# Attention of a hybrid decoder step: 160 transpose groups in 76 steps in place of 88, with a fifth copy buffer

## What is computed

```python
def nsa_core(q, qpos, gates, cmp_kv, fetch, n_sel, win_kv, win_pos):
    s = einsum(qg, cmp_kv[:, :, 0]) - slopes * d_c
    p_cmp = masked_softmax(s, d_c >= 0)
    o_cmp = einsum(p_cmp, cmp_kv[:, :, 1])
    ...
    _, idx = lax.top_k(score, min(TOP_K, n_sel))
    sel = fetch(idx)
    ...
    o_slc = einsum(masked_softmax(s, d_s >= 0), vsel)
    ...
    o_win = einsum(masked_softmax(s, mask_w), win_kv[:, :, 1])
    o = g[:, :, 0] * o_cmp + g[:, :, 1] * o_slc + g[:, :, 2] * o_win
```

## Time and profile before

| | us |
|---|---|
| median of 3 runs | 1759.17 |
| lowest and highest | 1758.44, 1761.16 |
| the profiled execution | 1755.95 |
| its span | 1754.3 |
| attention stage in the trace | 506 to 840.5 |
| matmuls busy in that stage | 315.5 of 334 |

### The profile page before, as it was taken

The page is one execution under the profiler, slowest core; times in us unless marked ns, Lnnn a source line. Parts: engine busy times, 40 slices in busy tenths (PEclk is TensorE's granted clock), DMA queues, the critical chain, the costliest instruction groups (busy, mean ns, idle before and its releaser), DMA issues.

```text
span 1754.3 us, 35862 instructions
## 1 busy us (share of the span) xinstructions
PE 1706.9 (97%) x13523; PEld 1584.2 (90%) x13523; DVE 1211.5 (69%) x1805; ACT 801.9 (46%) x1462; POOL 836.7 (48%) x862
## 2 busy tenths in 40 slices
PE   8999999999989999999999999999999999999998
PEld 7999998999966666667998999999999999999998
DVE  6789965879777677767548754455596979745435
ACT  5311325565876666667325333333433333315335
POOL 2202965555524343444454656665664545326521
PEclk9999999999999999999999999999999999999999
DMA  5323346655533443442414323332584643341114
GB/s 163 123 64 81 88 149 163 187 155 145 137 98 96 145 123 115 128 135 60 148 49 153 111 98 108 111 111 99 178 263 144 180 146 120 103 128 55 49 37 147
DMA packets 179723, 214.61 MB, mean 122 GB/s; under 512 B 22940, under 2 KB 150664, under 8 KB 174799
## 3 DMA queue, kind: packets, MB, share of 16 engines
q1 hardware_dynamic: 174333, 196.30, 36.4%
q0 software_dynamic: 4032, 13.40, 2.6%
q10 hardware_dynamic: 1186, 2.63, 0.5%
HBM read 181.30 MB, written 35.59 MB: 124 GB/s over the span
## 4 chain that ended last, share of the span: by engine, by line
PE 51%; DVE 9%; issue 3%; ACT 3%; DMA 2%; POOL 2%; SPq 1%; ACTq 0%; DVEq 0%; POOLq 0%
PE ps L2825 11%; PE ps L3208 6%; PE ps L2830 5%; PE ps L2583 5%; PE ps L201 3%; PE ps L3213 3%; PE ps L1984 3%; PE ps L1997 3%; PE ps L1970 3%; PE ps L3721 2%; DVE S L2238 2%; PE ps L2024 2%; POOL S L1924 2%; PE ps L207 2%; SPq L3083 1%
## 5 line engine op out<-in xcount | busy, mean ns | idle before, releaser
L1924 POOL TENSOR_SCALAR S<-S,inv,gate_p 128x640 f32<-128x640 f32 (+7 forms) x186 | 124.2, 684 | 187.3 <-DVE inv L2248 187.3
L1311 DVE SCALAR_TENSOR_TENSOR y<-u,conv_w,y 128x1024 f32<-128x1024 f32 x120 | 156.0, 1346 | 1.2
L3208 PE MATMUL ps<-dn_op_hi,dn_hi 128*128 128x264 f32 x672 | 136.8, 285 | 3.8 <-DVE dn_op_lo L3256 3.8
L3208 PE MATMUL ps<-dn_op_lo,dn_hi 128*128 128x264 f32 x672 | 135.7, 283 | 0.0
L659 POOL COPY relaid<-raw 128x512 f32<-128x512 f32 x128 | 83.5, 683 | 87.5 <-PE ps_p L1083 39.3
L2121 ACT ACTIVATE S<-S,mn 128x64 f32<-128x64 f32 (+8 forms) x180 | 108.7, 609 | 1.2 <-DVE mn L2238 1.2
L3139 POOL TENSOR_TENSOR dn_lo<-dn_t_sum,dn_hi 128x512 fp32r<-128x512 f32 x48 | 77.2, 1610 | 65.9 <-ACT dn_hi L3161 65.7
L3208 PEld LDWEIGHTS ps<-dn_op_hi,dn_hi 128*128 128x128 f32 x672 | 103.7, 188 | 5.3 <-DVE dn_op_lo L3256 5.1
L1012 PE MATMUL ps_p<-Ahi,win_hi 128*128 128x352 f32 x456 | 104.1, 328 | 1.5 <-DVE Alo L1288 1.5
L2825 PE MATMUL ps<-s_hi,up_hi 128*128 128x264 f32 x512 | 104.1, 285 | 0.0
L3208 PEld LDWEIGHTS ps<-dn_op_lo,dn_hi 128*128 128x128 f32 x672 | 103.9, 188 | 0.0
(11 more groups left out here) (494 smaller groups left out, 5052.1 us busy)
## 6 DMA issues: line engine op xcount, KB each, us to landing
s_raw<-in_cache_slc_kv_dram SPq DMA_DIRECT2D x256, 128.0 KB, 2.1
raw<-in_cache_cmp_kv_dram SPq DMA_DIRECT2D x188, 128.0 KB, 3.7
dn_op_raw<-hidden SPq DMA_DIRECT2D x21, 1056.0 KB, 6.5
hidden<-cs SPq DMA_DIRECT2D x32, 528.0 KB, 2.6
up_raw<-in_w_up_dram SPq DMA_DIRECT2D x16, 1024.0 KB, 5.4
dn_w<-in_w_down_dram SPq DMA_DIRECT2D x48, 256.0 KB, 4.9
win_raw<-in_w_in_dram SPq DMA_DIRECT2D x38, 256.0 KB, 3.3
raw<-in_cache_cmp_kv_dram POOLq DMA_DIRECT2D x64, 128.0 KB, 3.7
```

The lines of the kernel that those rows point to most:

```text
L1311: i = V_.scalar_tensor_tensor(out=y, in0=x, scalar=w, in1=y, op0=ALU.mult, op1=ALU.add)
L1924: nc.gpsimd.tensor_scalar(x, x, inv[:, n % 3, 3 * e + br:3 * e + br + 1], c.gate_p[:, i, H * br + h:H * br + h + 1], ALU.mult, ALU.mult).t ...
L3208: nc.tensor.matmul(ps[:, 2 * m + j, 0:HC], w_hi[q % 4][:, k, :], x[:, k, HC * j:HC * j + HC], start=(k == 0 and x is op_hi[n]), stop=False)
```

## The change

A unit of 5 or 7 groups (i = 3, 6 and 7) now ends in a step of three groups, so that its steps are 2+3 or 2+2+3. Units of 3 groups (i = 1) keep their 2+1. There are 76 steps. Since a step of three can follow one of two before its `pv` is done, there are five `PT` tiles, and the fifth lies where small sampled tiles were; some of these go to two free stretches of the memory. `START` becomes 4, 7, 11, 14, 18, 21, 25, 29, 32, 36, 39, 43, 47, 50, 54, 57, 61, 65, where it was 4, 8, 12, 16, 21, 25, 29, 34, 38, 42, 46, 51, 55, 59, 64, 68, 72, 77; the second choice of pages starts at step 28 in place of 34. The lines of `attend` behind the new function stand 9 lower.

```diff
+NPT = 5
...
+TABLES_FREE = RSTD_OFF + 3584
+CONV_FREE = AREA - 3712
...
-    PTs = [c.at(f"PT{s}", [P, 512], F32, PT_OFF + 2048 * s) for s in range(4)]
+    PTs = [c.at(f"PT{s}", [P, 512], F32, PT_OFF + (2048 * s if s < 4 else 24064)) for s in range(NPT)]
...
-    spot = [PT_OFF + 24064]
+    spot = [PT_OFF + 24064 + 2048]
...
-    score = sb("score", [P, 72])
-    left1 = sb("left1", [P, 72])
+    score = c.at("s_score", [P, 72], F32, TABLES_FREE)
+    left1 = c.at("s_left1", [P, 72], F32, CONV_FREE)
...
-    steps = [[m for m in range(a, min(a + 2, first_group[n + 1]))] for n in range(NU) for a in range(first_group[n], first_group[n + 1], 2)]
+
+    def cut(n):
+
+        size = first_group[n + 1] - first_group[n]
+        return [2] * (size // 2 - 1) + [3] if size % 2 and size > 3 else [2] * (size // 2) + [1] * (size % 2)
+
+    steps = [[first_group[n] + sum(cut(n)[:m]) + x for x in range(cut(n)[m])] for n in range(NU) for m in range(len(cut(n)))]
...
-                    mm = nc.tensor.matmul(ps_O[rows, 0:P], v, PTs[k % 4][:, at:at + P],
+                    mm = nc.tensor.matmul(ps_O[rows, 0:P], v, PTs[k % NPT][:, at:at + P],
```

More of the change, by code:

```diff
@@ L1738, in attend @@
     Snew = sb("Snew", [P, 2, P])
-    score = sb("score", [P, 72])
-    left1 = sb("left1", [P, 72])
+    score = c.at("s_score", [P, 72], F32, TABLES_FREE)
+    left1 = c.at("s_left1", [P, 72], F32, CONV_FREE)
     left2 = sb("left2", [P, 72])
-    top = sb("top", [P, 16])
-    block_at = sb("block_at", [P, 64])
-    selb = [sb(f"selb{gr}", [P, 64]) for gr in range(2)]
+    top = c.at("s_top", [P, 16], F32, TABLES_FREE + 640)
+    block_at = c.at("s_block_at", [P, 64], F32, CONV_FREE + 288)
+    selb = [c.at(f"s_selb{gr}", [P, 64], F32, TABLES_FREE + 288) if gr == 0 else sb(f"selb{gr}", [P, 64]) for gr in range(2)]
     win_at = sb("win_at", [P, 8])
     imp = sb("imp", [P, 64])
-    mx = sb("mx", [P, 16])
-    nm = sb("nm", [P, 4])
+    mx = c.at("s_mx", [P, 16], F32, TABLES_FREE + 544)
+    nm = c.at("s_nm", [P, 4], F32, TABLES_FREE + 608)
     alpha = sb("alpha", [P, 2])
@@ L2129, in keep @@
             w = kept_width(k)
-            nc.scalar.activation(PTs[k % 4][:, 0:w], bank(("p", k))[:, 0:w], ACT.Copy).then_inc(kept[0], 1)
+            nc.scalar.activation(PTs[k % NPT][:, 0:w], bank(("p", k))[:, 0:w], ACT.Copy).then_inc(kept[0], 1)
         def keep_keys(z, bb):
@@ L2251, in keep @@
             w = kept_width(k)
-            V_.tensor_copy(PTs[k % 4][:, 0:w], bank(("p", k))[:, 0:w]).then_inc(kept[1], 1)
+            V_.tensor_copy(PTs[k % NPT][:, 0:w], bank(("p", k))[:, 0:w]).then_inc(kept[1], 1)
         def keep_keys(z, bb):
```

## The result

The changed kernel takes 1765.5 us in the median (1763.2 to 1769.3, 7 runs) and the kernel before, run beside it on the same chip, 1758.4 (1754.7 to 1761.2, 7 runs). The ratio is **1.0048, with a 95% interval from 1.0039 to 1.0057**: slower by 8.4 us (0.0048 of 1758), or 7.1 by the two medians. But it stood on 1759.2 for the kernel before, where these runs show 1758.4; the predicted *change* of +4.1 us was about half of the real one.

The account below looks back on a forecast made before the run. PE, busy 97% of the span, was taken as the bound. Losses of 9.8 us less gains of 5.8 gave +4.0; 1759.2 + 4.1 gave 1763.3 us, range 1754 to 1770.

Parts of the forecast that it names:

- units 2 to 4: Scores moved behind unit 3's first turn, then a new 1.5 us POOL wait at unit 4: 2.4 us lost.
- pass g = 1, units 10 and 11: Quad's second half moves into unit 10's first step: 1.0 us less work before unit 11, 0.8 ahead of unit 10; 1.8 lost.
- pass g = 2, units 17 to 19: Two quad halves in a row at units 17 and 18, two bank waits near 2 us: 1.8 us lost.
- pass g = 3, units 26 to 28: Unit 26 waits 1.0 longer, unit 27 0.4 less, unit 28 repeats unit 4: 1.9 us lost.
- end, units 30 and 31: Less PE work before unit 31 while POOL's pair takes the same time, plus `mixA`: 1.9 us new idle.
- gains: Existing waits for weights, copied banks, `mixA` and scores get covered by longer steps or other work: 5.8 us won.
- The 0.5 at `mixA`: End of the stage: ACT, with `y_hi` and exponentials in the same steps, adds some 0.5 us at `mixA`.
- Wrong: waits in the i = 6 and 7 units, where I put none: Sign against the forecast: waits in units of i = 6 and 7, where it claimed none.
- Tiles at no cost: The fifth `PT` tile and the moved small tiles add no wait and cost nothing.
- Cancel: Rival: across the attention stage losses and gains cancel, within 3.5 us, near 1760 us; chance 0.32.
- Faster by the last unit's scaling: Rival: two `y_lo` move ahead of unit 31's `inv`, POOL done in 7.5 us, kernel 1754 us; chance 0.15.
- Doesn't do what it says: Rival: waits on a quad's pages, some us each; chance 0.13 together with the rival of DVE chains as the bound.
- chains as the bound: Rival: DVE chains bound i = 1 to 3, late copies stopping turns: +12, 1771 us; 0.13 together with the pages rival.

Follow-up runs that it names:

- `y_lo` late: Changed kernel with the last two of four `y_lo` subtractions on DVE moved to the last two steps: 1.0028 of the kernel before.
- size 5 alone: Changed kernel with steps of three groups only in the units with 5 groups, 84 steps: 1.0026 of the kernel before.
- chunk late: Changed kernel where units with 5 groups send out score chunks as one and then two, not two and then one: 1.0024 of the kernel before.
- quad early: Changed kernel with the sampled quad of unit 22 begun one step earlier: 1.0027 of the kernel before.
- the tiles alone: Changed kernel with five `PT` places and moved tiles kept, but the old 88 steps: 0.9999 of the kernel before.
- the control: Old 88 steps with five `PT` places and moved tiles, and the last two `y_lo` subtractions in the last two steps: 0.9994 of the kernel before.
- Size 7 alone: Changed kernel with steps of three groups only in the units with 7 groups, 80 steps: 0.9998 of the kernel before.

## Why the prediction was right in sign and short in size

By its own steps, in us of idle PE; measured values are the units' gaps in the first profile against before:

| step of the prediction | predicted | measured |
|---|---|---|
| units 2 to 4 | +2.4 | +2.2 |
| pass g = 1, units 10 and 11 | +1.8 | +1.4 |
| pass g = 2, units 17 to 19 | +1.8 | +1.9 |
| pass g = 3, units 26 to 28 | +1.9 | +1.3 |
| end, units 30 and 31 | +1.9 | +2.5 |
| gains | -5.8 | -4.4 |
| waits it did not have (units 6, 13, 15, 22) | 0 | +2.4 |
| sum | +4.0 | +7.3 |

- **Units 3 and 4.** Right in place and close in size: unit 4's turn waits 1.23 (predicted 1.5), the copied bank 0.45 (predicted 0.2), and the wait of 0.46 in the earlier trace rows is gone. Without the half-clock stretch (`y_lo` late) unit 3's first turn lies 10.21 us ahead of unit 4's, and PE is there after 8.99; predicted were 10.6 and 9.1. Unit 3's first turn still waited for POOL, now 1.06 against 0.94. The work taken from ahead of it did come back as idle time, but as a wait of 1.25 inside the keys' turns (0.60 in the second profile), for a copy that stands behind the sampled chain on DVE, and not as a longer wait for POOL. The experiment with size 5 alone has unit 4's 1.22 again, though its second quad begins a step later, so the step of three in the unit before makes it.
- **Middle passes.** Of g = 1, 0.8 was to lie ahead of unit 10 and 1.0 behind it. The first came, in its place (0.82, below), but the 1.25 of the earlier trace rows went with it and 0.34 came; unit 10's idle time is 1.28 as before (1.29). Unit 11 then waits 1.30 for POOL, the same mechanism as at unit 4. The prediction had kept the 10.48 us from unit 10 to 11; it was 9.85 (613.62 to 623.47). In g = 2 the "two bank waits near 2 us" are 1.20 and 1.89. In g = 3 unit 26 lost 0.22 and not 1.0, unit 27 gained 0.34, unit 28 has the 1.23 of unit 4.

```profile
613.62 1.06 PE L1993 MATMUL ps<-ident,S 128*128 128x128 f32 x8 [0.82 <-ACT s_KT L2142]
...
618.35 1.06 PE L2041 MATMUL ps<-s_KT,QB 128*32 128x512 f32 x8 [0.34 <-DVE mn L2247]
```

- **The end.** The wait became 2.90, inside the predicted 2 to 3. Of the reasons the subtractions were tested: moved away, they bring it to 1.00, near the 0.80 of before. The shorter distance wasn't tested by itself. The 0.5 at `mixA` came as 0.45 for a bank (835.48, `DVE PT`).
- **Gains: the term that was mis-sized.** The two waits of 0.96 and the three of 0.35 went (one of 0.34 came, at unit 10); units 12 and 20 together gave 2.6 with them. At unit 14 both booked waits went, and 0.52 for a bank came, so 0.6 is left. But the copied bank at unit 22 (0.61 in the earlier trace rows), booked as a gain, turned into the 1.94 us ahead of the quad's weights; and unit 17's 0.42 and 0.41 went only for the 1.20 counted under g = 2. The failing step is the sentence that a longer step covers such waits. It covers PE's side. It also fills all three banks at once, so that the next turn waits for the copy of the step's first group, and that copy stands behind everything that ACT or DVE already has there. I priced that only where I had a name for the queue. (This is unit 22; at units 6, 14 and 15 turns of `S` wait for ACT's copy of keys turned ahead of them.) "Wrong: waits in the i = 6 and 7 units, where I put none" was met: new waits for a bank stand in units 6, 14, 15, 22 and 30, of 0.51, 0.52, 0.41, 1.94 and 0.45.
- **Two terms were missing**, and it is luck that they hide each other. The clock was left out altogether (+4.0, or 3.6 by the measured stretch). And I let the 12 boundaries be worth nothing in themselves, where the same matmuls took 4.1 us less at full clock. The forecast of idle time (22.5) was 3.0 us short, and this is what the sum missed in the stage. Idle time is not the whole price.
- **Tiles at no cost**: right, 0.9999 of before.
- **Rivals.** *Cancel* fell: its losses of 5.8 were really 9.3. *Faster by the last unit's scaling* had the right mechanism in the wrong place: POOL is done in 6.74 us, even less than the 7.5 it named, but its first pair, which alone PE waits for, gained 0.19 (4.33 us to the turn, against 832.81 less 828.29, 4.52, before). The two subtractions that are left stand directly behind `inv`. *Doesn't do what it says* has no wait on pages to show. The 12 us of *chains as the bound* are not in the trace.

## What to carry to other kernels

An order with fewer and larger steps removes waits of the engine that bounds, and moves copies of the others to where they queue. Before merging a step, count the banks it fills, and list for each engine what stands ahead of the copy that frees the first of them; three groups filled three banks here, the first copy stood behind 3.3 us of exponentials, and the next turn waited 1.9 us. Look for what lies directly behind the event that releases the next stage (here the subtractions behind `inv`): freeing those 2 us took one line. And take the two halves of such a rule apart by size: one half was worth nothing by itself, 3.3 us with the line; the other cost 4.6. If another table hangs on the number of steps, as `START` does here, hold it fixed in one more kernel.

## What the runs showed of the hardware that I had not expected

- **Half-clock stretches are a price of the order, but not tied to a place in it.** Each lasts 3.4 us or 6.8 us at 0.50 to 0.51, and one of 3.4 costs 1.5. In the changed kernel those of the attention stage follow idle time: 506 stands at the 2.2 us wait of the stage's start, 534 behind 1.25 and 1.06, 759 behind 1.94 at unit 22. A second profile had all three within 0.7 us of their places. But with the same instructions and the same waits the kernel with `y_lo` late has none at 534 and 759, and one at 706 beside the 1.89 of unit 18, where the changed kernel has none (chunk late and quad early have one there too). The amount is steadier than the places. Busy time at half clock in the stage is 11.3, 16.1 and 8.8 us in the three profiles with the changed PE order (the third with `y_lo` late), and 3.2, 3.4, 5.0 and 4.7 in four with the old order (the kernel before twice, the tiles alone, the control). Over all executions the mean granted clock is 0.9937 in 7 of the changed kernel and 0.9959 in 79 of the kernel before, that is 22 and 14 us of the span at half clock. The 0.997 given with the profile before is such a mean: 11.2 us of that span were at 0.50, 0.6% of it, less than in most executions. What decides on a stretch is open, and it makes single profiles of small edits unreliable.
- **Changes of kind cost PE time without showing as idle.** A single turn between two other groups takes 0.26 us from start to start (538.50 to 538.76 in the earlier trace rows); as the ninth in a row it adds 0.11 (1.13 for nine from 540.52, 1.02 for eight from 545.03, above). Over the stage, starts across such a change lie 0.20 to 0.22 us apart, turns in a row 0.11 to 0.12, value products 0.055. Counted by the line of the matmul, PE's order has 363 changes before and 342 after; 21 times about 0.12 is an estimated 2.5 of the 4.1 us. The rest I can't assign. Size 7 alone has 18 changes fewer and saves 2.6 us, size 5 alone 4 fewer and 0.4.
- **Waits repeat to 0.02 us** from execution to execution (1.06, 1.22, 1.94 and 2.91 against 1.06, 1.23, 1.94 and 2.90), and so do the units' lengths (10.21 and 10.22 us for unit 3 in the two kernels without the stretch at 534), except next to a half-clock stretch: the bank wait of 1.25 was 0.60 behind the one at 523. So one profile is enough to price a wait, and not to price the kernel.
